# A hybrid encoder trunk on one core: products with the identity written as TensorE transposes

## The chip, the core and the metric

The kernel runs on one core of a Trainium2 chip. A core has five engines that take their instructions side by side and wait for each other through semaphores: TensorE (PE: matrix products, and a weight load for each), VectorE (DVE), ScalarE (ACT), GpSimd (POOL) and SyncE (SP, which starts most of the DMAs). The metric is the time of one execution on the device in microseconds, as the median of several runs. Before the change it is 3178.19 us (three runs, 3176.36 to 3195.85).

## The reference

Two layers run over 256 tokens with 2048 channels in float32. In each, one input projection feeds three mixers side by side (RWKV-7, gated DeltaNet, mLSTM), whose outputs go through one output projection; then come a convolved gated MLP and a gated per-layer embedding. Cut to what the change touches:

```python
def _rms_norm(x, g):
    xf = x.astype(jnp.float32)
    y = xf * lax.rsqrt(jnp.mean(xf * xf, axis=-1, keepdims=True) + EPS)
...
def _chunk_gated_delta(q, k, v, g, beta):          # second mixer
    g = jnp.cumsum(g.reshape(*lead, n, C), axis=-1)
    diff = g[..., :, None] - g[..., None, :]
    decay = jnp.where(incl, jnp.exp(jnp.where(incl, diff, 0.0)), 0.0)
    L = jnp.where(strict, jnp.einsum("...id,...jd->...ij", kb, k) * decay, 0.0)
...
def reference(x, p, ...):
    for i in range(DEPTH):
        u = _rms_norm(h, norm_mix[i])
        z = u @ w_in[i]
        y_rw = _rwkv7_mix(...)      # first mixer: values v go into a scan over the tokens
        y_gd = _gated_deltanet_mix(...)
        y_ml = _mlstm_mix(...)
        h = h + concatenate([y_rw, y_gd, y_ml]) @ w_out[i]
        u = _rms_norm(h, norm_ffn[i])
        h = h + (silu(gate) * val) @ w_down[i]     # gate, val: conv of u @ w_up[i]
        u = _rms_norm(h, norm_ple[i])
        h = h + sigmoid(u @ w_ple_gate[i]) * (p[i] @ w_ple_proj[i])
    return _rms_norm(h, norm_final)
```

## The kernel before

The code has one block for each engine, and the order of each engine's instructions is written out by hand; semaphores tie them together. There is no scheduler. Tokens stand in two tiles (NT = 2) of P = 128.

The large products (input, output, up, down and gate projections) stream their weights through a ring of four slots. ScalarE rounds a landed slot to `whi`, VectorE or GpSimd makes the rest `wlo`, and TensorE makes three products for each weight tile. They fill most of the time. `slot_wait` and `slot_done` carry the ring.

Two helpers write TensorE's instructions. `mm` (line 642) is an ordinary product; every operation made by it has line 643 in the profile. `turn` (line 645) is a transpose with the identity `ident` as the other operand; its operations have line 647. Both put their first operand in as weights, and in the profile the name of the moving operand stands first (`ps<-ident,gs`). Three places make float32 products with the identity, whose result is the transpose of the weights:

- `turn_scales` (line 793), called once in the input projection and once in the up projection of each layer. It turns a column of `small` (1/rms of each token), broadcast to 128 columns, into a tile in which each row holds the scales of all tokens. It stands between the products of a dense projection; ScalarE copies the tile (`rstd_row`).
- `rw_norms` (line 691), once for each of the four pairs of heads of the first mixer in each layer. Behind a product of squares with `headones` it turns the two value tiles of `zrw` (shown as Z in the profile), once with `ident` and once with `centre`, which also takes out the mean. ScalarE copies both results. The first call of a layer stands in the input projection; the other three stand in `keys_turned` of the pair before, between level 1 and level 2 of `invert`. Behind it come `keep_quarters_busy` products (`lev,one_h`), which here first wait for ScalarE's copy of the turned keys (KBt, semaphore `rw_scc`), and then level 2 (TN,scores).
- `decays` (line 1092), four calls of four products for each of the three pairs of heads of the second mixer (i = 0, 1, 2) in each layer. It broadcasts columns of `gs` into tiles of PSUM, from which VectorE subtracts a scalar (line 2194, `exponents`), and ScalarE takes the exponential. In the first pair `ml_back` follows (products of TN and TT with the identity, on 6 partitions), which waits for VectorE's running maxima (line 2122). In the other pairs, `decays(0, 1)` waits for a copy of ScalarE. Behind the decays stand the 4 score products (AR), four turned values (UA), and then `turn_out`, which waits until VectorE has normalised and gated the output of the pair before (YB, line 1887).

Of the kernel before, what the change touches and what calls it, by code (L numbers as in the profile page):

```python
# [28 lines left out]
P = 128  # L29
# [6 lines left out]
def trunk(nc, x, p, norm_mix, w_in, rw_shift_mu, rw_w0, rw_w2, rw_a0, rw_a2, rw_g2, rw_k_k, rw_k_a,  # L36
# [4 lines left out]
    T = x.shape[1]  # L41
    NT = T // P
    KT = D // P
    RW = rw_w0.shape[2]
    RC = RW // P
# [68 lines left out]
    with ExitStack() as ctx:  # L114
# [37 lines left out]
        ident = sb("ident", [P, P])  # L152
# [6 lines left out]
        centre = sb("centre", [P, P])  # L159
        one_h = sb("one_h", [P, P], BF16)  # L160
        epsb = sb("epsb", [P, 4])
        small = sb("small", [P, 16])
# [9 lines left out]
        gs = sb("gs", [P, 24, 2])  # L172
# [44 lines left out]
        zrw = zpart(3 * RC * T).rearrange("p (c t) -> p c t", t=T)  # L217
# [37 lines left out]
        ps = [ctx.enter_context(nc.psum_tensor(f"ps{i}", [P, 512], F32)) for i in range(8)]  # L255
# [378 lines left out]
        def _(pe):  # L634
# [7 lines left out]
            def mm(o_, a, b, start, stop):  # L642
                return pe.matmul(o_, a, b, start=start, stop=stop, skip_group_check=True)  # L643

            def turn(o_, a):
                n = a.shape[0]
                return pe.transpose(o_, a, ident[0:n, 0:n])  # L647
# [43 lines left out]
            def rw_norms(c, n, banks=(1, 5)):  # L691
                pe.wait_ge(S["rw_sq"], n + 1)
                mm(ps[banks[0]][:, 0:T], headones[:], ch[:, 2, :], True, True).then_inc(S["rw_ssq"], 1)
                for j, matrix in enumerate((ident, centre)):
                    for t in range(NT):
                        last = mm(ps[banks[1]][:, j * T + t * P:j * T + (t + 1) * P], zrw[:, c + 2 * RC, t * P:(t + 1) * P], matrix[:],
                                  True, True)
                last.then_inc(S["rw_vt"], 1)

            def rw_coefficients(n):  # L700
# [88 lines left out]
            for L in range(DEPTH):  # L789
# [3 lines left out]
                def turn_scales(q, bank):  # L793
                    pe.wait_ge(S["rstd_ready"], q)
                    for t in range(NT):
                        last = mm(ps[bank][:, t * P:(t + 1) * P], small[:, 4 + t:5 + t].to_broadcast([P, P]), ident[:], True, True)
                    last.then_inc(S["rep_psum"], 1)

                nb = pe.snap(L * NB)
# [32 lines left out]
                for i, (kind, b, c0, tiles) in enumerate(blocks):  # L832
# [8 lines left out]
                    for k in range(KSLOTS):  # L841
# [10 lines left out]
                        for c in range(len(tiles or ())):  # L852
                            off = 2 * RD * c if kind == "lora" else P * c
                            for kk in range(KS):
# [3 lines left out]
                                last = mm(ps[g + c][:, 0:T], lo, uhi[:, u, :], False, u == KT - 1)  # L858
                        for t in range(0 if tiles else NT):
                            w = width((kind, b, c0, tiles))  # L860
                            for kk in range(KS):
                                u = KS * k + kk
                                last = product(ps[g + t][:, 0:w], (uhi[:, u, t * P:(t + 1) * P], ulo[:, u, t * P:(t + 1) * P]),
                                               wparts(slot, kk, 0, w), u == 0, u == KT - 1)
# [137 lines left out]
                for j in range(2):  # L1002
                    for d in range(2):
                        for t in range(NT):
                            last = turn(ps[(1, 6)[j]][0:MH, d * T + t * P:d * T + (t + 1) * P],
                                        gy[:, 0, t, 2 * MH * j + MH * d:2 * MH * j + MH * d + MH])
# [79 lines left out]
                for i in range(GP):  # L1086
# [5 lines left out]
                    def decays(d, j):  # L1092
                        for h in range(2):
                            for t in range(NT):
                                o_ = slice((2 * h + t) * P, (2 * h + t + 1) * P)
                                row = (8 if j else 0) + 2 * t + d
                                last = mm((ps[2 + d] if j else ps[4 * d])[:, o_], gs[:, row, h:h + 1].to_broadcast([P, P]), ident[:],
                                          True, True)
                        last.then_inc(S["gd_gb"], 1)

                    decays(0, 0)
# [13 lines left out]
                    for h in range(2):  # L1115
                        for t in range(NT):
                            last = mm(ps[6 + h][:, t * T:(t + 1) * T], AR[h][:, t, 0, :], AR[h][:, t, :, :], True, True)
                    last.then_inc(S["gd_sc"], 1)
                    pe.wait_ge(S["gd_arg"], pe.snap(n2 * 2) + 2)
                    for h in range(2):  # L1120
                        for t in range(NT):
                            last = turn(ps[2][:, (2 * h + t) * P:(2 * h + t + 1) * P], chg[:, h, t * P:(t + 1) * P])
# [26 lines left out]
                    for d in range(2):  # L1149
# [5 lines left out]
                        for h in range(2):  # L1155
                            j = 2 * h + F
# [1270 lines left out]
```

## Time and profile before

| | us |
|---|---|
| median of 3 runs | 3178.19 |
| lowest, highest | 3176.36, 3195.85 |
| span of the profiled execution | 3174.6 |
| TensorE matmuls busy in it | 3054.9 |
| VectorE busy | 2081.5 |
| ScalarE busy | 1657.2 |
| GpSimd busy | 612.3 |

The profile is of one execution, and its times count from the start of its span. Busy time of TensorE is that of its matmuls; their weight loads are counted apart (PEld) and overlap them. A matmul's own duration is latency, and several are in flight at a time, so the cost of one in a row of them is read from the distance between their starts. A float32 product leaves more than one record. The granted clock (PEclk) is a share of 2.4 GHz; 0.50 is 1.2 GHz.

### The profile page before, as it was taken

To read this page: it belongs to the slowest core of one execution; us is meant where nothing else is said; L and a number is where in the kernel's file an instruction comes from. 1 tells how busy PE (TensorE), PEld (TensorE's weight loads), DVE (VectorE), ACT (ScalarE), POOL (GpSimd) and SP (SyncE) were. 2 spreads that over 40 slices of the span, in tenths; PEclk is the share of its full clock that TensorE was granted. 3 is DMA by queue.
4 is the path that set the end of the run, shared out by engine and by line. 5 is a ranking of instruction groups with operands and counts; after the bars stand their busy time and mean duration, and the time that the engine had idled before them with its cause. 6 is when DMAs were issued, how large, how long until landed. Compare 5 with 4: busy or idle time off the path is not lost.

```text
span 3174.6 us, 56293 instructions
## 1 busy us (share of the span) xinstructions
PE 3054.9 (96%) x20767; PEld 2626.2 (83%) x20767; DVE 2081.5 (66%) x3474; ACT 1657.2 (52%) x2673; POOL 612.3 (19%) x517
## 2 busy tenths in 40 slices
PE   8999988899999999999999999889899999999998
PEld 7899877777888888888788998777688888888886
DVE  6775655777777777455568655567767777774554
ACT  6555654456555555444455556545465555544444
POOL 2000453440212222000000005334402221220000
PEclk9999998999999999999999999999899999999999
DMA  6666101114656666666556660021256665666664
GB/s 208 185 180 187 47 2 59 61 55 146 195 185 192 192 182 196 221 195 191 164 169 194 183 178 15 2 66 55 67 178 193 184 192 181 196 198 215 193 183 152
DMA packets 265227, 479.22 MB, mean 151 GB/s; under 512 B 17314, under 2 KB 81148, under 8 KB 264380
## 3 DMA queue, kind: packets, MB, share of 16 engines
q1 hardware_dynamic: 265020, 476.48, 49.1%
q8 instruction: 128, 2.10, 0.3%
q14 instruction: 79, 0.65, 0.1%
HBM read 474.32 MB, written 2.10 MB: 150 GB/s over the span
## 4 chain that ended last, share of the span: by engine, by line
PE 87%; DVE 8%; ACT 1%; issue 1%; DVEq 1%; POOL 0%; SPq 0%; DMA 0%; ACTq 0%; POOLq 0%
PE ps L643 86%; PE ps L647 1%; DVE scores L2194 1%; DVE wlo L1801 1%; DVE XS L1851 0%; ACT L1272 0%; DVE upair L1814 0%; DVE TN L1860 0%; DVE AR L2221 0%; DVE H L1833 0%; ACT XS L1272 0%; DVE st L1875 0%; DVE TN L2246 0%; DVE heads L1880 0%; POOL H L580 0%
## 5 line engine op out<-in xcount | busy, mean ns | idle before, releaser
L1801 DVE TENSOR_TENSOR wlo<-ring,whi 128x1024 fp32r<-128x1024 f32 (+4 forms) x905 | 1095.6, 1229 | 672.2 <-ACT whi L1272 666.3
L643 PE MATMUL ps<-upair,whi 128*128 128x512 f32 x4032 | 1404.4, 394 | 6.3 <-DVE upair L1814 5.7
L1272 ACT ACTIVATE whi<-ring 128x1024 fp32r<-128x1024 f32 (+4 forms) x947 | 941.0, 1002 | 795.6 <-PE ps L643 715.8
L643 PE MATMUL ps<-upair,wlo 128*128 128x256 f32 x4032 | 1121.2, 278 | 0.0
L643 PEld LDWEIGHTS ps<-upair,whi 128*128 128x128 f32 x4032 | 756.5, 188 | 182.9 <-issue 6.1
L643 PEld LDWEIGHTS ps<-upair,wlo 128*128 128x128 f32 x4032 | 758.9, 188 | 0.3 <-issue 0.2
L643 PE MATMUL ps<-whi,upair 128*128 128x390 f32 (+2 forms) x1280 | 367.5, 364 | 0.0
L625 POOL TENSOR_TENSOR YB<-YB 128x1024 f32<-128x1024 f32 x22 | 125.3, 5697 | 828.9 <-DVE YB L1824 828.9
L643 PE MATMUL ps<-whi,ghi 128*128 128x512 f32 x704 | 274.4, 390 | 0.0
L643 PE MATMUL ps<-whi,glo 128*128 128x512 f32 x704 | 274.0, 389 | 0.0
L643 PE MATMUL ps<-wlo,ghi 128*128 128x512 f32 x704 | 273.9, 389 | 0.0
L643 PEld LDWEIGHTS ps<-whi,upair 128*128 128x128 f32 x1280 | 237.0, 188 | 24.5 <-issue 4.6
L643 PE MATMUL ps<-wlo,upair 128*128 128x390 f32 (+2 forms) x640 | 230.3, 360 | 0.0
L502 POOL TENSOR_TENSOR YB<-YB 128x256 f32<-128x256 f32 x8 | 6.4, 804 | 959.2 <-PE ps L643 930.4
L643 PEld LDWEIGHTS ps<-whi,ghi 128*128 128x128 f32 x704 | 132.2, 188 | 27.3
L643 PEld LDWEIGHTS ps<-wlo,ghi 128*128 128x128 f32 x704 | 132.2, 188 | 27.3
L643 PEld LDWEIGHTS ps<-whi,glo 128*128 128x128 f32 x704 | 132.2, 188 | 27.2
L643 PEld LDWEIGHTS ps<-wlo,upair 128*128 128x128 f32 x640 | 120.4, 188 | 11.5 <-issue 1.9
L574 POOL TENSOR_TENSOR wlo<-ring,whi 128x1024 fp32r<-128x1024 f32 x42 | 99.5, 2369 | 132.7 <-DVE st L1875 76.1
L643 PE MATMUL ps<-whi,yhi 128*128 128x512 f32 x256 | 115.7, 452 | 3.2 <-issue 2.9
L643 PEld LDWEIGHTS ps<-TN,scores 64*64 64x64 f32 x2464 | 91.1, 143 | 24.1 <-issue 15.7
L643 PE MATMUL ps<-TN,XS 64*64 64x64 f32 x2240 | 93.1, 225 | 18.4 <-DVE XS L1851 16.1
(311 smaller groups left out, 3621.5 us busy)
## 6 DMA issues: line engine op xcount, KB each, us to landing
ring<-in_w_up_dram SPq DMA_DIRECT2D x352, 512.0 KB, 3.9
ring<-in_w_down_dram SPq DMA_DIRECT2D x176, 512.0 KB, 4.3
ring<-in_w_in_dram SPq DMA_DIRECT2D x128, 384.0 KB, 3.5
ring<-in_w_out_dram SPq DMA_DIRECT2D x64, 512.0 KB, 3.7
ring<-in_w_ple_gate_dram SPq DMA_DIRECT2D x64, 512.0 KB, 4.4
ring<-in_w_in_dram SPq DMA_DIRECT2D x51, 512.0 KB, 4.5
ring<-in_w_in_dram SPq DMA_DIRECT2D x64, 390.0 KB, 3.5
ring<-in_w_in_dram SPq DMA_DIRECT2D x32, 396.0 KB, 3.6
```

The source lines that it names most:

```text
L502: pool.tensor_tensor(ch[:, 4, :], ch[:, 1, :], ch[:, 3, :], ALU.mult)
L574: pool.tensor_tensor(wlo[:, slot % RING, :, :], ring[:, slot % RING, :, :], whi[:, slot % RING, :, :].bitcast(F32), ALU.subtract).then_inc ...
L625: pool.tensor_tensor(up_buf(0), up_buf(0), up_buf(1), ALU.mult)
L643: return pe.matmul(o_, a, b, start=start, stop=stop, skip_group_check=True)
L647: return pe.transpose(o_, a, ident[0:n, 0:n])
L1272: return act.activation(o_, i_, f, **kw)
L1801: v.tensor_tensor(wlo[:, slot % RING, :, 0:w], ring[:, slot % RING, :, 0:w], whi[:, slot % RING, :, 0:w].bitcast(F32), SUB).then_inc(S["lo ...
L2194: last = v.tensor_scalar(scores[d][:, j, u, :], ps[2 + d if j else 4 * d][:, u * P:(u + 1) * P], gs[:, 8 + 2 * t + d, h:h + 1], 0.0, SUB, MIN)
```

## The change

The products with the identity in the three places are written with `turn` where they were written with `mm`. In `rw_norms` the loop over the two matrices becomes two loops over the token tiles, the first with `turn` and the second, unchanged, with `mm` and `centre`. The identity products of `ml_back` stay as they are.

```diff
@@ rw_norms
-                for j, matrix in enumerate((ident, centre)):
-                    for t in range(NT):
-                        last = mm(ps[banks[1]][:, j * T + t * P:j * T + (t + 1) * P], zrw[:, c + 2 * RC, t * P:(t + 1) * P], matrix[:],
-                                  True, True)
+                for t in range(NT):
+                    turn(ps[banks[1]][:, t * P:(t + 1) * P], zrw[:, c + 2 * RC, t * P:(t + 1) * P])
+                for t in range(NT):
+                    last = mm(ps[banks[1]][:, T + t * P:T + (t + 1) * P], zrw[:, c + 2 * RC, t * P:(t + 1) * P], centre[:],
+                              True, True)
                 last.then_inc(S["rw_vt"], 1)
@@ turn_scales
                     for t in range(NT):
-                        last = mm(ps[bank][:, t * P:(t + 1) * P], small[:, 4 + t:5 + t].to_broadcast([P, P]), ident[:], True, True)
+                        last = turn(ps[bank][:, t * P:(t + 1) * P], small[:, 4 + t:5 + t].to_broadcast([P, P]))
                     last.then_inc(S["rep_psum"], 1)
@@ decays
                                 row = (8 if j else 0) + 2 * t + d
-                                last = mm((ps[2 + d] if j else ps[4 * d])[:, o_], gs[:, row, h:h + 1].to_broadcast([P, P]), ident[:],
-                                          True, True)
+                                last = turn((ps[2 + d] if j else ps[4 * d])[:, o_], gs[:, row, h:h + 1].to_broadcast([P, P]))
                         last.then_inc(S["gd_gb"], 1)
```

No instruction moves on any engine. Here is the place on TensorE in the first mixer where the value tiles are turned between two levels of the inversion, in order of issue, with the line of before and that of the change (KB are keys, Z the values; here x2 counts the two calls of the code, one for each token tile, and not the records that the profile shows):

```order
 L647 MATMUL ps<-ident,KB_105 128x128 x2
 L643 MATMUL ps<-YB,headones 128x256
-L643 MATMUL ps<-ident,Z 128x128 x2
+L647 MATMUL ps<-ident,Z 128x128 x2
 L643 MATMUL ps<-centre,Z 128x128 x2
 L643 MATMUL ps<-lev_67,one_h 64x256 x2
```

The two products become two transposes at the same place, and the work around them keeps its order. The other two places read in the same way.

## Rows read from the trace of the kernel before

**Rows 1.** The page: busy time of the engines, and the chain by engine.

```profile
PE 3054.9 (96%) x20767; PEld 2626.2 (83%) x20767; DVE 2081.5 (66%) x3474; ACT 1657.2 (52%) x2673; POOL 612.3 (19%) x517
...
PE 87%; DVE 8%; ACT 1%; issue 1%; DVEq 1%; POOL 0%; SPq 0%; DMA 0%; ACTq 0%; POOLq 0%
```

**Rows 2.** Groups by shape, TensorE: out<-in, shape, count | busy, mean ns | idle before.

```profile
L643 PE MATMUL ps<-ident,gs 128*128 128x128 f32 x192 | 23.5, 277 | 1.4 <-ACT lnp L1272 1.4
...
L643 PE MATMUL ps<-ident,Z 128*128 128x128 f32 x32 | 4.9, 274 | 0.0
...
L647 PE MATMUL ps<-ident,UA 128*128 128x128 f32 x24 | 3.7, 277 | 0.0
...
L643 PE MATMUL ps<-ident,small 128*128 128x128 f32 x16 | 2.4, 273 | 0.0
```

**Rows 3.** Timeline of TensorE at 41 and 736 us: start, us, operation, count.

```profile
41.38 0.60 PE L643 MATMUL ps<-ident,small 128*128 128x128 f32 x4
...
42.05 0.28 PE L643 MATMUL ps<-upair,wlo 128*128 128x256 f32 x1
...
736.53 1.03 PE L647 MATMUL ps<-ident,H 128*128 128x128 f32 x8
...
737.64 0.39 PE L643 MATMUL ps<-wlo,yhi 128*128 128x512 f32 x1
```

**Rows 4.** Timelines at 363 and 465 us, three engines; idle before in brackets.

```profile
362.67 0.39 ACT L1272 ACTIVATE KBt<-ps 128x256 f32<-128x256 f32 x1
...
363.25 0.30 PE L643 MATMUL ps<-lev,one_h 64*64 64x256 bf16 x2
...
364.06 0.42 DVE L1851 TENSOR_TENSOR XS<-ps,lev 128x256 f32<-128x256 f32 x1 [1.49 <-PE ps L643]
...
464.96 0.38 ACT L1272 ACTIVATE KBt<-ps 128x256 f32<-128x256 f32 x1
...
465.39 0.30 PE L643 MATMUL ps<-lev,one_h 64*64 64x256 bf16 x2 [0.66 <-ACT KBt L1272]
```

**Rows 5.** Timeline of TensorE and VectorE, second mixer, first pair.

```profile
503.03 3.73 PE L643 MATMUL ps<-ident,gs 128*128 128x128 f32 x32
508.59 1.05 PE L643 MATMUL ps<-ident,TN 6*128 6x6 f32 x8 [1.82 <-DVE TT L2122]
509.50 1.72 PE L643 MATMUL ps<-ident,TT 6*128 6x6 f32 x8
...
512.80 2.14 DVE L2194 TENSOR_SCALAR scores<-ps,gs 128x128 f32<-128x128 f32 x8
```

**Rows 6.** Timeline of TensorE, second mixer, second pair.

```profile
578.51 2.94 PE L643 MATMUL ps<-ident,gs 128*128 128x128 f32 x24 [0.34 <-ACT lnp L1272]
581.29 1.89 PE L643 MATMUL ps<-AR 128*128 128x256 f32 x8
583.02 0.60 PE L647 MATMUL ps<-ident,UA 128*128 128x128 f32 x4
586.89 1.09 PE L647 MATMUL ps<-ident,YB 128*128 128x128 f32 x8 [3.27 <-DVE YB L1887]
```

**Rows 7.** The chain that ended last, over the same stretch: start, us, what.

```profile
579.62 1.04 DVE scores L2194 x4
...
586.08 0.76 DVE YB L1887 x2
...
590.16 9.42 PE ps L643 x56
```

**Rows 8.** Stretches: length, busy PE, PEld, DVE, ACT, POOL; granted clock; DMA.

```profile
509.70:519.80 10.10, 6.89 (x24) 5.75 (x24) 7.92 (x29) 3.71 (x7) 3.63 (x6) 0.50 0.71 237
...
591.60:595.00 3.40, 3.40 (x9) 2.64 (x8) 3.09 (x8) 0.06 (x1) 0.64 (x2) 0.50 0.02 5
```

**Rows 9.** Timeline of TensorE at the start of the program, and at 589 us.

```profile
8.49 2.98 PE L647 MATMUL ps<-ident,H 128*128 128x128 f32 x13 [8.49 <-DVEq L1774]
...
12.01 0.77 PE L647 MATMUL ps<-ident,heads 128*128 128x128 f32 x5 [0.22 <-DMA heads<-in_rw_shift_mu_dram]
...
589.66 0.42 PE L647 MATMUL ps<-ident,AR 128*128 128x128 f32 x1
```

## The prediction, made before the changed kernel was run

> **What bounds the kernel now.** I read the page first. Its first block shows TensorE's matmuls busy for 96% of the span of 3174.6 us, and the chain that ended last runs through TensorE for 87% of it, VectorE for 8% and ScalarE for 1% [rows 1]. So time taken off TensorE may come off the end, but only where TensorE is the one that others wait for. The groups by shape come next, because they price the changed operations and give their number. Then each place where a changed operation stands is looked at in the timeline, to see whether TensorE waits right behind it.
>
> **What one operation costs.** The groups by shape count matmul records [rows 2]. The decay broadcasts (ps<-ident,gs) are 6 pairs of heads (3 in each layer) times 16 products, 96 products, and show 192 records. Likewise 16 value turnings show 32 records and 8 scale rows show 16. The turnings already written as transposes (line 647) show one: UA is 6 times 4 transposes and 24 records. So a float32 product with the identity is two passes, and a float32 transpose is one. Both kinds of record last about 275 ns, but that is latency, and what counts is the distance between starts. For products, 32 records take 3.73 us [rows 5]: (3.73 - 0.275) / 31 = 0.111 us for a pass, 0.223 us for a product. For transposes, 4 UA records take 0.60 us [rows 6]: (0.60 - 0.273) / 3 = 0.109 us for a whole transpose. Nothing in these rows shows a transpose whose operand is a broadcast column. As products, the broadcast column (gs, small) and the plain tile (Z) differ by no more than 4 ns [rows 2], so I take 0.109 us for both; the bounds are 0.109 us and, if a broadcast operand gave up the whole gain, the 0.223 us of now.
>
> The Trainium skill weighs this differently: "TensorE: Matmul & The Clock Gate", section Terms, in its entry on the xbus, calls the transpose mode of trn2 four times faster for float32. By that, a transpose would cost a quarter of a product, 0.056 us, and the dense saving below would be about 2.0 us where the rows give 1.3. The trace has the duration, half and not a quarter, so the rows decide.
>
> Over all 120 converted operations that is 120 x (0.223 - 0.109) = 13.7 us less TensorE work, 0.4% of the span. The question is how much of it was waited for.
>
> **Part by part.**
>
> Scale rows, 4 calls of 2 products, and the first value turning of each layer, 2 calls of 2. They stand in the dense input and up projections, between products that follow each other without a gap. Around a scale-row call, the way from its first record to the second projection product behind it is 42.05 - 41.38 = 0.67 us for 4 passes; around 8 transposes in the output projection it is 737.64 - 736.53 = 1.11 us [rows 3]. Taking 8 x 0.109 off the one and 4 x 0.111 off the other leaves 0.24 and 0.23 us, so returning from transposes to products costs what returning from a product costs, and no switching price has to be added. Each call saves 2 x (0.223 - 0.109) = 0.23 us, and 6 calls 1.4 us. Nothing hides TensorE here, so it comes off the end.
>
> The other 6 value turnings (3 in each layer) stand between two levels of the inversion of the previous pair. VectorE waits 1.49 us there for TensorE [rows 4], so TensorE is on the path. But the work behind the turnings, the keep-busy products at 363.25, also waits for ScalarE's first copy of KBt, which ends at 362.67 + 0.39 = 363.06. In the last pair, which has no value turning, that copy ends at 464.96 + 0.38 = 465.34 and the keep-busy products start 0.05 us later, at 465.39 [rows 4]. With the turning 0.23 us shorter, TensorE would be ready at 363.02, the copy lets it go at 363.11, and 363.25 - 363.11 = 0.14 us is gained. Six times that is 0.8 us. What is late next is that copy of ScalarE, which does not depend on the turning.
>
> The decay broadcasts, 96 of the 120 and 10.9 us of the 13.7, stand at six places and I cost them all at nothing. In the first pair of each layer TensorE makes 16 products at 503.03 and is done at 506.76; then it waits 1.82 us for VectorE's running maxima (TT, line 2122) until 508.59 [rows 5]. The change makes it done 1.8 us earlier and the wait 3.6 us long. The first reader of a decay tile, VectorE at line 2194, starts at 512.80, long after [rows 5]. In the other two pairs 4 products come before a wait for ScalarE and 12 behind it (578.51 to 581.45). Behind them stand 8 products AR, 4 turnings, and then a wait of 3.27 us for VectorE's normalised output YB, until 586.89 [rows 6]. The chain over this stretch is VectorE's: from scores at 579.62 over YB at 586.08 up to 590.16, where TensorE takes over again [rows 7]. Twelve products save 12 x 0.114 = 1.4 us, which lengthens the 3.27 us wait to 4.6. If VectorE were not the cover, each of these four places would give up to 1.8 us and the first ones as much again, which is the second rival below.
>
> Sum: 1.4 + 0.8 + 0 = 2.2 us off the profiled 3174.6, 3172.4 us. The runs shown have a median of 3178.19, 3.6 us above that span, so the measured time would be about 3176.0 us. No wait, no DMA and no order on any engine changes.
>
> **The clock.** Longer idle stretches could cost clock. After the 1.82 us wait above, TensorE is granted half clock (1.2 GHz) from 509.70 to 519.80, and after the 3.27 us wait it is at 0.50 from 591.60 to 595.00 [rows 8]. The change puts more idle time ahead of both. If the clock fell earlier, before the products TN and TT at 508.59, the first 8 would take 1.7 us and not 1.05, as the TT rows behind them do [rows 5], 0.7 to 0.9 us on VectorE's path, once in each layer. In the other pairs the 8 turnings of YB (1.09 us at full clock) would take about 0.9 us longer, mostly beside VectorE's scores. The bounds are 0 and 2 x 0.9 + 4 x 0.9 = 5.4 us.
>
> **The rivals.**
>
> *As summed*, -2.2 us, 3176.0: chance 0.55.
>
> *The clock falls earlier around the decays*, up to 5.4 us against the 2.2: between 3176 and 3181, no change that can be told. For it: the clock already falls there. Against: an earlier fall may also bring an earlier return. Chance 0.28.
>
> *The decays are on the path after all*: 13.7 us gone, 3164.5. The two waits for VectorE behind them [rows 5, 6] speak against it, and nothing for it but TensorE's share of the chain. Chance 0.05.
>
> *The change does not do what it says*: a transpose of a broadcast column runs as slowly as the product. The 16 value turnings alone are left, 0.5 + 0.8 = 1.3 us: 3177. Chance 0.08.
>
> *Slower*: transposes do not hold the clock as products do. The place is the run of small products in the first mixer and around the decays. Price: from 509.70 to 519.80 TensorE is busy 6.89 us at half clock [rows 8], which is 3.4 us of work at full clock, so one such stretch loses 3.4 us if all of it is waited for. One more at each of the 12 places (6 of decays, 6 value turnings between levels) loses 41 us: 3178.2 - 2.2 + 41 = 3217. It decides from 10 such stretches on (34 us less the 2.2 saved). Against it: at the start of the program TensorE did nothing but transposes from 8.49 on. The first 13 are (2.98 - 0.42) / 12 = 0.213 us apart (0.42 us is the last one's own length, that of the transpose at 589.66 in a half-clock stretch), and 5 more at 12.01 are (0.77 - 0.27) / 4 = 0.125 us apart [rows 9]: the distance of half clock first, that of nearly full clock later, with nothing but transposes between. Chance 0.04.
>
> The Trainium skill speaks for this last rival: "TensorE: Matmul & The Clock Gate", section Part 4: PE-mode transpose, says that transpose-mode work does not count as busy in the way that brings the full clock. The trace disagrees at the one place where it can be seen.
>
> **How the numbers follow.** The time is that of the likeliest case, 3176.0 us. The range has to take in the clock case (3181), the weak-transpose case (3177) and the runs' own spread around the median; I let it run from 3167 to 3187, which leaves out the decays on the path and the slow clock, and about one chance in ten of a disturbed median. A measurement of this kernel can tell about 1%, 32 us. Only the slow-clock rival ends beyond that, and even the whole 13.7 us stay within: faster 0.01, within 1% 0.96, slower 0.03.
>
> **What would show it.** In the profile after, the group ps<-ident,gs should be at line 647 with 96 records where there were 192, Z 16 and small 8; starts 0.109 us apart; the wait for VectorE before YB in the second and third pair 4.6 us where it was 3.27, and the wait behind the first pair's decays 3.6 where it was 1.82. The keep-busy products behind a value turning should start 0.05 us behind ScalarE's first KBt copy. The prediction is wrong if a transpose of a broadcast column is further than 0.12 us from the next, if the wait before YB stays at 3.3 us while the pair gets shorter, or if the granted clock is at half in stretches in which it was full.

## The result, and the profile of the changed kernel

The changed kernel takes 3194.36 us (median of 8 runs, 3186.32 to 3197.18), the kernel before 3178.27 us in as many runs beside it (3176.36 to 3195.85). The ratio is 1.0037 (95% interval 1.002 to 1.0053): slower by 0.4%, where 3176.0 us had been forecast and 3187 was the end of the range. It is within the 1% that had been given 0.96, but above the range.

The page of the changed kernel's profiled execution, for [rows 1]: its span, busy time of the engines, and the granted clock in 40 slices.

```profile
span 3195.0 us, 56053 instructions
PE 3069.8 (96%) x20647; PEld 2624.7 (82%) x20647; DVE 2063.9 (65%) x3474; ACT 1657.5 (52%) x2673; POOL 614.3 (19%) x517
PEclk9999998999999999999999999999899999999999
```

Against a span of 3174.6 us before, 20.4 us are to be found. The groups by shape, for [rows 2] (count | busy us, mean ns of one | idle before):

```profile
L643 PE MATMUL ps<-upair,whi 128*128 128x512 f32 x4032 | 1426.8, 399 | 6.2 <-DVE upair L1814 5.6 <-DVE wlo L1801 0.5
...
L643 PE MATMUL ps<-upair,wlo 128*128 128x256 f32 x4032 | 1132.1, 281 | 0.0
...
L647 PE MATMUL ps<-ident,gs 128*128 128x128 f32 x96 | 13.6, 293 | 3.2 <-ACT lnp L1272 3.2
...
L647 PE MATMUL ps<-ident,Z 128*128 128x128 f32 x16 | 3.1, 273 | 0.0
...
L647 PE MATMUL ps<-ident,small 128*128 128x128 f32 x8 | 1.5, 270 | 0.0
```

The converted groups are as foretold: line 647, half the records. Two groups that the diff does not touch have grown. These are the same two groups of the kernel before:

```profile
L643 PE MATMUL ps<-upair,whi 128*128 128x512 f32 x4032 | 1404.4, 394 | 6.3 <-DVE upair L1814 5.7 <-DVE wlo L1801 0.5
...
L643 PE MATMUL ps<-upair,wlo 128*128 128x256 f32 x4032 | 1121.2, 278 | 0.0
```

They are the projections' main products: activations (upair) with the high and the low half of the weights, 512 columns and 256 in turn, 4032 of each. What is the time between their starts? Two stretches inside the up projections answer it, far from every converted operation. The columns are those of [rows 8]. First the kernel before, then the changed one:

```profile
800.00:1200.00 400.00, 400.00 (x2310) 349.81 (x2309) 300.66 (x378) 214.96 (x299) 94.34 (x27) 1.00 0.61 189
2400.00:2800.00 400.00, 400.00 (x2310) 349.65 (x2309) 300.78 (x379) 215.12 (x299) 94.39 (x27) 1.00 0.61 190
```

```profile
800.00:1200.00 400.00, 400.00 (x2265) 346.91 (x2265) 288.32 (x374) 210.47 (x294) 94.21 (x27) 1.00 0.60 185
2400.00:2800.00 400.00, 400.00 (x2265) 346.82 (x2265) 286.97 (x369) 211.38 (x295) 90.31 (x27) 1.00 0.60 187
```

TensorE is busy for the whole of both, at granted clock 1.00 (2.4 GHz) in both, and the DMA share differs by 0.01 (189 and 190 GB/s against 185 and 187, as the stream is slower). Yet 400 us hold 1155 pairs before and 1132.5 after: 400 / 1155 = 0.3463 us a pair, 400 / 1132.5 = 0.3532. **The same instructions on the same tiles follow each other 6.9 ns a pair further apart, 2%.** (A record counts that lies only partly in the stretch, so both are a few tenths of a nanosecond too small; by the starts the difference is 6.6 ns.) The starts make the difference visible. TensorE's timeline at 1000 us (start, length in us), before and after:

```profile
999.65 0.39 PE L643 MATMUL ps<-upair,whi 128*128 128x512 f32 x1
999.88 0.27 PE L643 MATMUL ps<-upair,wlo 128*128 128x256 f32 x1
999.99 0.40 PE L643 MATMUL ps<-upair,whi 128*128 128x512 f32 x1
...
1000.69 0.40 PE L643 MATMUL ps<-upair,whi 128*128 128x512 f32 x1
```

```profile
999.80 0.40 PE L643 MATMUL ps<-upair,whi 128*128 128x512 f32 x1
1000.04 0.28 PE L643 MATMUL ps<-upair,wlo 128*128 128x256 f32 x1
1000.16 0.40 PE L643 MATMUL ps<-upair,whi 128*128 128x512 f32 x1
...
1000.51 0.40 PE L643 MATMUL ps<-upair,whi 128*128 128x512 f32 x1
...
1000.86 0.40 PE L643 MATMUL ps<-upair,whi 128*128 128x512 f32 x1
...
1001.22 0.40 PE L643 MATMUL ps<-upair,whi 128*128 128x512 f32 x1
```

Three pairs take 1000.69 - 999.65 = 1.04 us before and 1000.86 - 999.80 = 1.06 after. Averaged over ten pairs, the distance is about 346.7 ns in the one rhythm and 353.3 in the other, with hardly anything between. I call them quick and slow from here on. In nanoseconds, the starts in the two traces show that these are two repeating patterns and not one pattern stretched. From 900 to 1200 us the quick one repeats every two pairs (350, then 343 or 344 ns: 693.4 in all), the slow one every three (350, 361, 349 ns: 1060 in all; the last four whi rows above are 0.35, 0.35 and 0.36 us apart). So an average over ten pairs of the slow one is 353.0 or 354.1 ns, as the tenth falls. Neither drifts into the other in these stretches; one goes on until something interrupts the stream. Over the 18 profiles of this study an up projection takes either 489.8 to 490.5 us (19 of them) or 499.1 to 499.7 (17), and nothing between.

By stages (us from the start of one to the start of the next):

| stage | before | after | difference |
|---|---|---|---|
| start and input projection, layer 0 | 345.89 | 348.76 | +2.87 |
| first mixer, layer 0 / 1 | 157.14 / 156.42 | 156.09 / 157.03 | -1.05 / +0.61 |
| second mixer, layer 0 / 1 | 250.35 / 250.39 | 249.85 / 250.66 | -0.50 / +0.27 |
| up projection, layer 0 / 1 | 490.32 / 490.32 | 499.15 / 499.15 | +8.83 / +8.83 |
| from the down projection to the input projection of layer 1 | 346.6 | 346.6 | 0 |
| input projection, layer 1 | 326.35 | 326.82 | +0.47 |
| end | | | +0.1 |

The two up projections carry 17.7 of the 20.4 us. In the input projections the stretch from the scale rows to the last pair before other products follow is 2.4 us longer in layer 0 (150.35 us for 147.96) and 0.7 in layer 1 (148.64 for 147.96), where another interruption ends the slow rhythm at 1682 us. Another 0.7 us lies ahead of the first scale rows, which start at 42.06 us and not at 41.38, and is not the change's as far as can be seen. From the scale rows at 771.8 to 1243.7 us there is room for 472 / 0.3467 = 1361 pairs; at 353.3 - 346.7 = 6.6 ns each that is 9.0 us, for the 8.83 found.

Where does the rhythm begin? In the kernel before, right behind the scale rows. TensorE's timeline there, in the first up projection:

```profile
771.79 0.60 PE L643 MATMUL ps<-ident,small 128*128 128x128 f32 x4
772.15 0.47 PE L643 MATMUL ps<-upair,whi 128*128 128x512 f32 x1
772.46 0.28 PE L643 MATMUL ps<-upair,wlo 128*128 128x256 f32 x1
772.58 0.40 PE L643 MATMUL ps<-upair,whi 128*128 128x512 f32 x1
...
775.70 0.39 PE L643 MATMUL ps<-upair,whi 128*128 128x512 f32 x1
```

From 772.58 to 775.70 are 9 pairs: 0.3467 us each. The changed kernel, same place:

```profile
773.10 0.38 PE L647 MATMUL ps<-ident,small 128*128 128x128 f32 x2
773.23 0.48 PE L643 MATMUL ps<-upair,whi 128*128 128x512 f32 x1
773.55 0.28 PE L643 MATMUL ps<-upair,wlo 128*128 128x256 f32 x1
773.67 0.40 PE L643 MATMUL ps<-upair,whi 128*128 128x512 f32 x1
...
775.79 0.40 PE L643 MATMUL ps<-upair,whi 128*128 128x512 f32 x1
```

Here 773.67 to 775.79 are 6 pairs, 0.3533 us each. Ahead of the call both kernels are in the slow rhythm. All four scale-row calls of the kernel before (41, 772, 1612 and 2342 us) have the slow rhythm ahead and the quick one behind. All four after (42, 773, 1622 and 2353 us) have the slow one ahead and behind. The foretold local saving did come: from the first record of the call to the second product behind it is 773.55 - 773.10 = 0.45 us, where it was 772.46 - 771.79 = 0.67. It gained 0.22 us, and the stream behind it lost 8.8.

### The profile page after: what moved, and what is told of

It reads as the page before. It is cut to its first block, busy times and chain, and to the rows that moved or that the text cites. A ratio compares the mean times of both kernels' runs of the same rounds, so it can differ in the third digit from the quotient of the medians.

```text
span 3195.0 us, 56053 instructions
## 1 busy us (share of the span) xinstructions
PE 3069.8 (96%) x20647; PEld 2624.7 (82%) x20647; DVE 2063.9 (65%) x3474; ACT 1657.5 (52%) x2673; POOL 614.3 (19%) x517
## 4 chain that ended last, share of the span: by engine, by line
PE 88%; DVE 8%; ACT 2%; issue 1%; DVEq 1%; POOL 0%; SPq 0%; DMA 0%; ACTq 0%; POOLq 0%
PE ps L643 86%; PE ps L647 1%; DVE wlo L1801 1%; DVE XS L1851 0%; ACT L1272 0%; DVE upair L1814 0%; DVE TN L1860 0%; DVE scores L2194 0%; DVE AR L2221 0%; DVE H L1833 0%; ACT XS L1272 0%; DVE st L1875 0%; DVE TN L2246 0%; DVE heads L1880 0%; POOL H L580 0%
## 5 line engine op out<-in xcount | busy, mean ns | idle before, releaser
L1801 DVE TENSOR_TENSOR wlo<-ring,whi 128x1024 fp32r<-128x1024 f32 (+4 forms) x905 | 1077.9, 1206 | 711.4 <-ACT whi L1272 703.7
L643 PE MATMUL ps<-upair,whi 128*128 128x512 f32 x4032 | 1426.8, 399 | 6.2 <-DVE upair L1814 5.6
```

What stands on the lines that cost most here:

```text
L1801: v.tensor_tensor(wlo[:, slot % RING, :, 0:w], ring[:, slot % RING, :, 0:w], whi[:, slot % RING, :, 0:w].bitcast(F32), SUB).then_inc(S["lo ...
```

## The experiments

**Theory R, as it stood first.** The passes (one for each record) between two stretches of projection products decide which rhythm the stream falls into: products give the quick one, the scale rows as two transposes leave the slow one. **Rivals:** the granted clock (half clock for 155.0 us of the span after, 139.1 before); the decays; the number of passes rather than their kind.

**1. The scale rows alone, either way.** In the changed kernel they become products again; in the kernel before they alone become transposes (the same line, reversed).

```
-   last = turn(ps[bank][:, t * P:(t + 1) * P], small[:, 4 + t:5 + t].to_broadcast([P, P]))
+   last = mm(ps[bank][:, t * P:(t + 1) * P], small[:, 4 + t:5 + t].to_broadcast([P, P]), ident[:], True, True)
```

> The changed kernel with its 4 scale-row calls (8 operations) written as products again; the 96 decay broadcasts and 16 value turnings stay transposes. Theory 'rhythm': in the profile of before the pairs of the dense projections (whi product to wlo product to next whi product) repeat every 346.7 ns from 42 to 224 us, from 773 us to the end of the up projection and from 1613 and 2343 us on, each time starting right behind a scale-row call of 4 product passes; in the changed kernel they repeat every 353.3 ns there, behind 2 transposes. So the products should bring back 346.7 ns and 3174 to 3179 us. Rival 'decays': the loss comes from the clock around the decays, then this stays at 3190 to 3197 us. Rival 'placement': any kernel whose instruction stream differs from before loses it; then it stays near 3194 us too, at 353.3 ns.

> The kernel before with nothing but its 4 scale-row calls written as transposes. Rhythm: 3192 to 3198 us and 353.3 ns a pair in both up projections. Decays: 3174 to 3179 us, since the decays are products as before.

Products back: 3177.86 us (10 runs, 3174.34 to 3195.39), ratio 0.9985 (0.9967 to 1.0003). Both up projections of its profile are quick. These are its two stretches, the matmuls on upair alone (length, busy PE with their number, granted clock, DMA):

```profile
800.00:1200.00 400.00, 400.00 (x2310) 1.00 0.61 189
2400.00:2800.00 400.00, 400.00 (x2309) 1.00 0.61 189
```

Transposes alone: 3186.15 us (10 runs, 3177.44 to 3198.52), ratio 1.0014 (0.9996 to 1.0033). Its profile has one up projection in each rhythm:

```profile
800.00:1200.00 400.00, 400.00 (x2310) 1.00 0.61 189
2400.00:2800.00 400.00, 400.00 (x2266) 1.00 0.61 186
```

So turning back 8 of the 120 operations takes the loss away: about 16 us between the medians of two kernels that have the other 112 as transposes (not run side by side; the ratios to the kernel before beside each are 1.0037 and 0.9985). The opposite edit gives at most half of it, with an interval that takes in 1, and that was a miss: scale rows as transposes do not always have the slow rhythm behind them. Experiment 4 finds out why.

The runs of the kernel before show the same thing. They gather around 3178, 3187 and 3196 us. The profiled executions say what these clusters are. With both up projections quick, the nine profiled executions of eight kernels took between 3175.98 and 3178.90 us; with one, 3184.66 (this one); with none, five took between 3196.77 and 3198.27 (the kernels of experiment 3, which have more operations, aside). No execution of the kernel before in an upper cluster was profiled, so for that kernel it is an inference. Counting runs, I put the bounds at 3182.5 and 3192; eight of the 100 runs of the kernel before lie between 3182 and 3184.5, so a count is good to a few runs only. Of the 100 runs of the kernel before in all jobs, 47 lie below the lower and 6 above the upper; of the changed kernel 0 and 5 of 8; of products back 8 and 1 of 10; of transposes alone 3 and 3 of 10. Two things follow. One program, the kernel before, has all three clusters, so the placing of instructions does not decide which. And the 8 runs beside the changed kernel were a lucky draw (6 of 8 in the lowest cluster, 41 of the other 92): the median of all 100 is 3183.4 us, so the change costs about 11 us against what the kernel before usually takes, and 16 against those 8.

**2. Mixed calls.** In the changed kernel, the first of a scale row's two operations a transpose and the second a product; then the other order; then an extra product or an extra transpose behind the two transposes.

```
    # turn, product
+   if t == 0: last = turn(...)
+   else:      last = mm(..., ident[:], True, True)
    # product, turn: the same with "if t == 1"
    # product behind (after both turns)
+   last = mm(ps[bank][:, T:T + P], small[:, 4:5].to_broadcast([P, P]), ident[:], True, True)
    # three turns
+   last = turn(ps[bank][:, T:T + P], small[:, 4:5].to_broadcast([P, P]))
```

> The changed kernel, but each scale-row call is one transpose and then one product (3 passes where before had 4 and the changed kernel 2). Rhythm set by what stands last: a product as the last operation gives 346.7 ns and 3174 to 3179 us. Rhythm set by the length of the interruption: 3 passes are neither, so some calls may land on 346.7 and others on 353.3 ns, 3178 to 3194 us.

> The changed kernel with each scale-row call as one product and then one transpose: the same 3 passes as the kernel with the transpose first, in the other order. If what counts is that a product stands last, this falls back to 3186 to 3197 us; if what counts is the length of the interruption (3 passes), it stays at 3171 to 3180 us as that one did.

> The changed kernel with one more product with the identity behind the 2 transposes of each scale-row call (its result goes to unused columns of the bank): 4 passes as before, and a product last. Rhythm, by either rule: 346.7 ns, 3174 to 3179 us. Decays or placement: about 3194 us.

> The changed kernel with one more transpose of the first scale column behind the 2 of each scale-row call, into unused columns: 3 passes, all of them transposes. At the 22 sites put in so far 2 transposes left 346.7 ns behind none, 2 products behind 7, a transpose and a product behind 14. If the number of passes decides, this is like the kernels with 3 passes: 3171 to 3180 us in most runs. If transposes as such hold the slow rhythm, it stays at 3186 to 3197 us in nearly all.

| kernel | median us (lowest to highest), 10 runs each | ratio to before (95%) | below 3182.5 / between / above 3192 |
|---|---|---|---|
| turn, product | 3177.01 (3170.86 to 3179.56) | 0.9978 (0.9964 to 0.9993) | 10 / 0 / 0 |
| product, turn | 3180.57 (3170.57 to 3198.18) | 0.9991 (0.9972 to 1.001) | 6 / 2 / 2 |
| turn, turn, product | 3182.58 (3171.90 to 3196.39) | 0.9997 (0.998 to 1.0013) | 5 / 4 / 1 |
| turn, turn, turn | 3194.31 (3184.51 to 3198.08) | 1.0023 (1.0006 to 1.004) | 0 / 3 / 7 |

A third transpose makes three passes of about the same length as a transpose and a product (which is two passes, [rows 2]); the one kernel is never quick throughout in 10 runs and the other always. In the profile of three turns both up projections are slow (2266 matmuls in either 400 us). So the number of passes is not it. Product, then transpose fell between its two expectations, with runs in all three clusters. But "a product somewhere in the call gives the quick rhythm" is not the rule either: with the product last but behind two transposes it does so in 5 runs of 10, where I expected nearly all.

**3. Many places in one kernel.** So few calls say little of how often each rhythm follows. In the changed kernel, 22 block starts of the input projection (11 in each layer) get two operations whose result is overwritten; they cost time and are only there to interrupt the stream.

```
    slot_wait(base, slot)
+   if tiles and i and k == 0:
+       turn(ps[g][:, 0:P], ident[:])      # or mm(ps[g][:, 0:P], ident[:], ident[:], True, True)
+       turn(ps[g][:, 0:P], ident[:])      # or mm(...)
```

> The changed kernel with 2 transposes of the identity put in front of the first weight tile of every block of the input projection that repeats the pair whi, wlo, except the first block of each layer: 11 sites a layer, 22 in all; their result is overwritten. It is read from the trace, site by site, which rhythm stands before and which behind. Rhythm set by the kind of interruption: 2 transposes leave 353.3 ns standing at nearly all sites (as the scale rows of the changed kernel do). Rhythm a matter of chance: behind each site either value, whatever was put in. The time itself is the changed kernel's plus 22 x 0.22 = 5 us, about 3199 us.

> The same 22 sites with 2 products with the identity (4 passes). Rhythm set by the kind: 346.7 ns behind nearly all sites of the input projection, which gains up to 6.6 ns for each of about 530 pairs a layer, 3.5 us a layer, against 22 x 0.45 = 10 us put in. By chance: either value behind each site, as often as with 2 transposes.

> The same 22 sites with one transpose and one product (3 passes), the form whose four scale-row calls gave the fast time in 10 runs of 10. Rhythm set by the kind: 346.7 ns behind nearly all sites, more surely than with 2 products (whose kernel had 2 slow runs in 10). By chance: as the other two.

The quick rhythm stands behind 0 of the 22 places with two transposes (two of them were entered quick), behind 7 with two products and behind 14 with transpose and product (5 of 11 in layer 0, 9 of 11 in layer 1). One run each: 3203.14, 3202.93 and 3197.88 us. The order of the three is that of theory R, but nearly all had been expected quick behind both forms with a product, and two products have far fewer than the four of four that they had as scale rows. So the place, or what the stream was doing ahead of it, matters too.

**4. What the call finds.** Read again with the rhythm ahead of each call written beside that behind it (averages over ten pairs), the profiles so far fit one rule at the scale rows, **theory K**: two transposes *keep* the rhythm they find, two products *change* it into the other, a transpose and then a product *set* the quick one. In the profile of transposes alone, the first two calls were entered at 346.6 and 346.7 ns and left at 346.6 and 346.7, the other two entered at 354.1 and left at 353.1: kept four times. That theory says the opposite of theory R once the call is entered quick. To force this, one transpose and one product more are put a slot (3.1 us) ahead of the scale rows of each up projection, in the changed kernel; the scale rows there then have four forms.

```
    # up projection, opening
+   if opening and g == 0 and k == 5:
+       pe.wait_ge(S["rstd_ready"], L * 3 + 2)
+       turn(ps[7][:, T:T + P], small[:, 4:5].to_broadcast([P, P]))
+       mm(ps[7][:, T:T + P], small[:, 4:5].to_broadcast([P, P]), ident[:], True, True)
    if opening and g == 0 and k == 6:
        turn_scales(L * 3 + 2, 7)
```

> The changed kernel, with one transpose and one product more a slot (some 3 us) ahead of the scale rows of each up projection; the scale rows stay two transposes. Theory K (two transposes keep the rhythm that they find, two products change it into the other, a transpose and a product set the quick one): the extra pair sets the quick rhythm, the scale rows keep it, both up projections run at 346.7 ns a pair; 3194.4 - 2 x 8.8 + 2 x 0.33 = 3177.5 us, nearly every run below 3182.5. Theory R (transposes leave the slow rhythm behind them): both at 353.3 ns, 3195 us.

> The same extra pair, but the scale rows of the up projections are two products, as in the kernel before. Theory K: the quick rhythm set by the extra pair is changed into the slow one; 353.3 ns a pair in both up projections, 3195 us, nearly every run above 3192. Theory R (products give the quick rhythm back): 346.7 ns, 3178 us.

> The same extra pair, the scale rows of the up projections product first, transpose second. Theory K, from the one profile in which such calls kept what they found in four places of four: the quick rhythm is kept, 3177.7 us. Theory R: between 3178 and 3195, as mixed as without the extra pair (6 of 10 runs quick throughout).

> The same extra pair, the scale rows of the up projections two transposes with one product more behind them. Theory K, from the one profile in which such calls changed what they found in four places of four: the quick rhythm is changed into the slow one, 3196 us. Theory R: mixed, as without the extra pair (5 of 10 runs quick throughout), about 3182 us.

| scale rows behind the extra pair | median us (lowest to highest), runs | ratio to before (95%) | below 3182.5 / between / above 3192 |
|---|---|---|---|
| turn, turn | 3176.61 (3172.29 to 3179.53), 10 | 0.9976 (0.9964 to 0.9989) | 10 / 0 / 0 |
| product, product | 3196.11 (3193.74 to 3199.02), 10 | 1.0036 (1.0021 to 1.005) | 0 / 0 / 10 |
| product, turn | 3176.46 (3174.12 to 3181.39), 9 | 0.9977 (0.9964 to 0.999) | 9 / 0 / 0 |
| turn, turn, product | 3196.92 (3196.09 to 3199.66), 6 | 1.0045 (1.0028 to 1.0062) | 0 / 0 / 6 |

All 35 runs fell as theory K says, and theory R falls. The rule had been read off earlier profiles; these four forms, each entered quick, are its test. Stretches in the up projections, the matmuls on upair alone (columns as above), first for turn, turn and then for product, product behind the extra pair:

```profile
800.00:1200.00 400.00, 400.00 (x2310) 1.00 0.60 189
2400.00:2800.00 400.00, 400.00 (x2310) 1.00 0.60 189
```

```profile
800.00:1200.00 400.00, 400.00 (x2266) 1.00 0.60 185
2400.00:2800.00 400.00, 400.00 (x2267) 1.00 0.61 187
```

The first is quick with the transposes of the change in place, the second slow with the products of the kernel before: the change's sign is turned round by what the call finds. Over all profiles of this study, at the scale rows and the extra pair (by averages over up to ten pairs ahead and behind; 349 ns right behind an extra pair counts as quick, since the first pair behind it is included):

| form | calls | found quick, left | found slow, left |
|---|---|---|---|
| two transposes | 30 | 13, all quick | 17, all slow |
| three transposes | 4 | 1, quick | 3, slow |
| product, turn | 6 | 3, quick | 3, slow |
| two products | 14 | 3, slow | 11, quick |
| turn, turn, product | 6 | 3, slow | 3, quick |
| turn, product | 20 | 3, quick | 17, quick |

No call of the 80 is an exception. Elsewhere there are: at the 22 places of experiment 3, two transposes entered quick were left slow twice, two products entered slow were left slow ten times, and a transpose and a product left the slow rhythm in 8 places. So the rule holds for the scale rows' place in the stream and can't be carried over as it is.

**5. The decays alone.** The kernel before, with only the 96 decays as transposes:

```
-   last = mm((ps[2 + d] if j else ps[4 * d])[:, o_], gs[:, row, h:h + 1].to_broadcast([P, P]), ident[:], True, True)
+   last = turn((ps[2 + d] if j else ps[4 * d])[:, o_], gs[:, row, h:h + 1].to_broadcast([P, P]))
```

> The kernel before with nothing but the 96 decay broadcasts written as transposes. Prediction on record: their 10.9 us lie under waits for VectorE, so the second mixer takes as long as before (within 1 us a layer), with half clock granted earlier in the first pair, up to 0.9 us a layer on the path. Rhythm: the dense projections are as in the kernel before, 3176 to 3196 us with about half the runs below 3182. Rival: if decays were what made the changed kernel slow, this has nearly all runs above 3186 us.

3179.12 us (7 runs, 3177.87 to 3187.61), ratio 0.9985 (0.9964 to 1.0005). Both stretches are quick (2309 and 2310 matmuls). The second mixer of layer 0, for this kernel and then for the one before:

```profile
504.94:755.57 250.63, 220.73 (x1953) 178.97 (x1952) 185.93 (x471) 125.83 (x217) 101.03 (x80) 0.90 0.23 75
```

```profile
503.03:753.38 250.35, 224.11 (x2001) 183.68 (x2000) 185.84 (x472) 125.60 (x218) 100.11 (x80) 0.91 0.24 75
```

TensorE has 3.4 us less to do and the stage is 0.28 us longer, not shorter. That is less than the same code differs by: with the decays as products, this stage took 250.35 and 250.39 us in the kernel before and 249.16 and 250.42 in that of transposes alone. What can be read is that the 5.5 us a layer (48 x 0.114) that the decays save TensorE did not come off. This kernel has half clock for 156.3 us, as much as the changed one, and its two up projections are quick: the clock is not what made the change slow.

**6. A version that keeps the gain.** Transpose, product again (the same kernel, 5 more runs), and with one transpose and one product more at the start of the low-rank block of the input projection, where the kernel before falls back into the slow rhythm:

```
+   if kind == "lora" and k == 0:
+       turn(ps[g][:, 0:P], ident[:])
+       mm(ps[g][:, 0:P], ident[:], ident[:], True, True)
```

> The changed kernel with each scale-row call as a transpose and then a product, word for word the kernel that had 10 fast runs of 10, with more runs. If that form nearly always leaves 346.7 ns, 9 in 10 runs are below 3182 us again and the ratio to before is 0.997 to 0.999. If it was luck (the same form left it at 14 of 22 sites), 3 to 6 in 10 runs are above 3182 us, as in the kernel before.

> The kernel before this one with a transpose and a product of the identity put in at the start of the block of the input projection at 224 us, from which the pairs run at 353.3 ns until 270 us in every profile so far. If they land on 346.7 ns, about 130 pairs a layer gain 6.6 ns each, 0.9 us a layer for 0.33 us put in: 1 us in all, 3170 to 3178 us in fast runs. If not, 0.7 us slower.

Again: 3174.73 us (5 runs, 3171.47 to 3175.98), ratio 0.9952 (0.9936 to 0.9967); with the 10 above, 15 runs of 15 below 3182.5. Its timeline at the call behind which the slow rhythm has gone over into the quick one:

```profile
771.45 0.27 PE L647 MATMUL ps<-ident,small 128*128 128x128 f32 x1
771.56 0.39 PE L643 MATMUL ps<-ident,small 128*128 128x128 f32 x2
771.70 0.47 PE L643 MATMUL ps<-upair,whi 128*128 128x512 f32 x1
...
772.12 0.40 PE L643 MATMUL ps<-upair,whi 128*128 128x512 f32 x1
...
775.94 0.39 PE L643 MATMUL ps<-upair,whi 128*128 128x512 f32 x1
```

From 772.12 to 775.94 are 11 pairs, 0.3473 us each. This kernel beats both. Against the quick runs alone of the kernel before in the same jobs (medians 3179.26 and 3177.59) its medians are 2.2 and 2.9 us lower. The forecast would be 2.2 - 4 x 0.114 = 1.7 us for this form; the runs do not show which parts the gain comes from. The rest of its gain is that no run, by its time, has a slow up projection. The second edit gives 3177.63 us (6 runs, 3174.57 to 3179.16), ratio 0.997 (0.9951 to 0.9988), 2.9 us more than the kernel without it beside it, where 0.7 had been expected for a failure: behind the new place only layer 1 turned quick (at 1796.7 us), layer 0 stayed slow: another exception away from the scale rows.

## Why the prediction was wrong, and where it was right

**The step that failed** is the one on the scale rows: -0.9 us, with the sentence that no switching price has to be added. It compared the first 0.24 us behind a call of products and behind transposes, in [rows 3], and found them equal. They are. But the stream behind a call was assumed to run on in the same way whatever the call's form. It runs at one of two speeds for the next hundreds of microseconds: the slow one is found by all four calls of the profile before, its two products change it into the quick one, and two transposes keep it. The term measured +17.7 us in the two up projections and +3.1 us in the input projections (2.4 and 0.7), the saved passes included, for the -0.9 forecast. The evidence for transposes there was also taken from the output projection, with other products behind it (wlo times yhi), where neither kernel differs. The spacing of the main products was never looked at, though [rows 3] stood in it. No rival named a lasting effect; they were about the clock, about who waits and about the price of one transpose. The range took the run of 3195.85 us for a disturbance, and by the clusters it was most likely this effect. The forecast's base, a median of 3178.19 us, was one of the lowest cluster too. (A slip without weight: the dense saving is given once as 1.3 us and once as 1.4; it is 12 x 0.114 = 1.37.)

**Price of an operation: right.** One record each. The 0.109 us for a broadcast operand can be read from TensorE's timeline in the decays-only kernel:

```profile
505.06 1.91 PE L647 MATMUL ps<-ident,gs 128*128 128x128 f32 x16
...
510.61 1.05 PE L643 MATMUL ps<-ident,TN 6*128 6x6 f32 x8 [3.65 <-DVE TT L2121]
```

(1.91 - 0.275) / 15 = 0.109 us, and the wait behind is 3.65 us, for the 3.6 foretold [rows 5]. So the rival of a weak broadcast transpose falls. The quarter of a product that "TensorE: Matmul & The Clock Gate" of the Trainium skill gives in its section Terms is not seen here: it is half.

**Value turnings between levels: the mechanism right, the gain small.** As foretold, the keep-busy products start 0.05 us behind ScalarE's first KBt copy. Timeline of the changed kernel, for [rows 4]:

```profile
364.24 0.38 PE L647 MATMUL ps<-ident,Z 128*128 128x128 f32 x2
364.46 0.61 PE L643 MATMUL ps<-centre,Z 128*128 128x128 f32 x4
364.65 0.39 ACT L1272 ACTIVATE KBt<-ps 128x256 f32<-128x256 f32 x1
365.09 0.30 PE L643 MATMUL ps<-lev,one_h 64*64 64x256 bf16 x2
```

The copy ends at 365.04. VectorE's wait for TensorE behind it is 1.36 us, for 1.49 before: 0.13 us, for the 0.14 foretold. The stage does not show it: the first mixers differ by -1.05 us in layer 0 and +0.61 in layer 1, and the kernels that have the value turnings as products differ among themselves by as much (156.29 to 157.33 us), so 0.8 us for six of them can't be read off the end.

**Decays at nothing: right** as far as experiment 5 can tell. In the changed kernel the wait before YB is 4.49 us, for 4.6 foretold [rows 6].

**The clock rival: right in what happens, wrong in the price.** The clock falls earlier. Timeline of the changed kernel, and the stretch of its first pair (columns as [rows 8]):

```profile
504.85 3.15 PE L647 MATMUL ps<-ident,gs 128*128 128x128 f32 x16
509.97 1.14 PE L643 MATMUL ps<-ident,TN 6*128 6x6 f32 x8 [1.97 <-DVE TT L2122]
...
588.26 1.97 PE L647 MATMUL ps<-ident,YB 128*128 128x128 f32 x8 [4.49 <-DVE YB L1887]
```

```profile
504.00:508.00 4.00, 4.00 (x18) 3.14 (x16) 3.78 (x6) 3.91 (x6) 2.75 (x4) 0.58 0.01 2
```

The eight YB turnings take 1.97 us for the 1.09 of before [rows 6], the half clock's distance, and the first decays of layer 0 are partly at half clock too, so that the wait behind them is 1.97 us and not 3.6. That half clock begins at 504.0 us, ahead of the decays, and neither layer 1 nor the decays-only kernel has it, so it is not the decays' doing. The turnings and the decays both lie beside VectorE's work, and the second mixers differ by -0.50 and +0.27 us: no price that can be told from 0, where up to 5.4 had been allowed. By the prediction's own sign (half clock in stretches in which it was full) it was wrong here as well, without loss of time. The slow rival's rule, that transposes don't bring the full clock ("TensorE: Matmul & The Clock Gate", section Part 4: PE-mode transpose, in the Trainium skill), foretold a slower kernel, but not for this reason: where the 8.8 us are lost the granted clock is 1.00 throughout.

**Settled, and open.** Shown: the loss sits in the spacing of unchanged products; the scale rows' form together with the rhythm they find decides it; the second operation of each call as a product again, or the quick rhythm set ahead of it, removes it. It also explains why scale rows as transposes alone were milder (their profile found the quick rhythm twice, the changed kernel's never) and would explain why the kernel before has clusters (a call that finds the quick rhythm changes it into the slow one, as in one call of the decays-only profile: 346.6 to 353.0 ns). Not shown: what makes two patterns of two and of three pairs, in TensorE or in what feeds it, and what keeps them going, what decides the rhythm ahead of the call, and why other places in the stream follow another rule. Why the whole change finds the slow rhythm nearly always (0 of 8 runs quick throughout, against 3 of 10 for the scale rows alone) is open too.

## What to carry to other kernels

An instruction inserted in a dense stream has two prices: its own distance, and the spacing of everything behind it. Count the stream's records in equal windows in both kernels; a 2% difference at full clock and full busy share is invisible in both shares, and here was 9 us a stage. And where a kernel's runs fall into clusters, find out what the clusters are before working out a gain smaller than their distance: here it was by all signs the same effect, in sight in the runs of the kernel before (3176.36 to 3195.85 us).

## What the runs showed of the hardware that was not expected

- Products of 512 and 256 float32 columns in turn, each with its own weight load, have two stable spacings at granted clock 1.00: 346.7 ns or 353.3 ns a pair. The first is a pattern of two pairs (350 and 343.4 ns), the second one of three (350, 361 and 349 ns). Each lasts up to hundreds of microseconds, and two to four passes between them (0.22 to 0.45 us) can change one into the other.
- At one place in the stream the effect of the interruption followed a rule in 80 calls of 80: two or three transposes, or a product and a transpose, kept the rhythm; two products, or two transposes and a product, changed it; a transpose and a product set the quick one.
- A transpose of a float32 128x128 operand is 0.109 us behind the last, whether the operand is a tile or one broadcast column; a product with the identity is 0.223.
- More half clock need not cost its share of time: the decays-only kernel has 156.3 us of it against 139.1 before, and the median of its quick runs is 3178.69 us against 3177.59 beside it.
